# Gate columns of linear attention in the narrow token-major product; index keys and attention keys projected by one tile

## The chip, the cores and the metric

The kernel runs on 1 core of one Trainium2 chip. The metric is the device time of one execution in microseconds (us). Three runs of the kernel before gave 2982.54, 2981.31 and 2982.35 us, median 2982.35.

## What is computed

One transformer block over 2048 tokens of width 1024. What matters here is its first half, cut to the lines that count:

```python
a = rms_norm(h, g_mix)
(gq, gk, gv, gg, ga, dq, dk, dv, iq, ik, iw, sq, sk, sv) = split(a @ w_in)   # 2520 columns
# gla: ga has 16 columns a token and goes through a small matrix to the decay
log_a = log_sigmoid(ga @ w_alpha2 + b_alpha) / GLA_TAU
# dsa: for every block of 128 queries, the 256 keys with the best index score
rel = relu(einsum('bthd,bsd->bths', iq, ik)); score = einsum('bth,bths->bts', iw, rel)
_, sel = top_k(score, 256)
logits = einsum('bthd,btkd->bhtk', dq, dk[sel]) + bias        # softmax, times dv[sel]
# swa: a window of 128 keys, with sq, sk, sv
h = h + concat([gla, dsa, swa]) @ w_out
```

`ik` and `dk` have 64 columns each and are one vector per token, shared by all heads. A mixture of experts and a gated embedding follow; the change doesn't touch them.

## The kernel before, in words

**First stage, `project_and_select` (lines 112 to 858).** TensorE (PE) makes `a @ w_in` as a list of products, `products` (lines 196 to 201). A product ("f", m, c) is feature-major: weight tile m (up to 128 columns of `w_in`, stationary) against a chunk c of 512 tokens of the transposed activations `aT` (moving), 8 matmuls over the depth, into one of two PSUM buffers `psP`. A product ("t", ...) is token-major: 128 tokens stationary, weight columns moving. The first 36 products (tiles `FIRST`, and the narrow product of 200 columns: `dv`, `iw`, `sv`) go chunk by chunk. Then come the tiles `LATER` (11 tiles, 4 chunks each, 44 products), then 32 token-major products of 256 columns (`gv` for 16 token tiles, then `gg`). Tile 0 holds the 64 index-key columns twice, tile 5 the 64 attention-key columns twice, so that each key lies in both partition halves (the matmuls at lines 697 and 1398 use a half for each of two heads). Tile 15 is the gate tile: 16 columns.

ScalarE (ACT) copies each product out of PSUM (lines 540 to 557): keys to `kI` and `kA` in SBUF, the others to `stage`, from where SyncE (SP) stores them to `proj_f` or `proj_t` in HBM. Product i waits until product i - 2 is copied (line 657).

Between products PE runs the **score pieces** ("R", line 697): index queries against `kI`, up to 512 keys. ACT applies relu (line 567) and the two head weights (line 581), GpSimd (POOL) adds (lines 495 and 498). There are 152 pieces; from product 18 on up to 5 of them follow each product.

VectorE (DVE) finds each query's 256th score by a **bit search**, four query blocks at a time, in four groups: 31 steps, each counting the scores above a threshold (lines 766 to 797). In the second half of group 2 and in all steps of group 3, ACT counts for two of the four blocks (`sense`, lines 592 and 596, item "C"); DVE then waits for ACT's count at line 794. The order of ACT's copies, pieces and counts is written out in advance by `deal()` (lines 263 to 342) from a table of costs. Then `select` (lines 841 to 849) makes the mask, and POOL stores it to HBM (line 529). After all products PE, ACT and the ACT queue make six tiles of the gated embedding ("embed", lines 713, 722, 626, 628, 630), and SP loads what the second stage needs (`MixerLoads.ahead`, lines 909 to 938), into the SBUF region `home` in which `aT` had been.

**Second stage, `mixers` (lines 945 to 1680).** One list of items for all engines, merged from three streams: sparse attention (`stream_a`), window attention (`stream_w`) and linear attention (`stream_g`), each spread evenly over the same number of slots. Item ("g", r, 0) multiplies the gate columns of 512 tokens (`low`, 16 partitions, loaded by `load_g`, line 920) by `w_alpha`; the rest of `g` computes decays. PSUM use goes round five banks, `psX`.

Of the kernel before, what the change touches and what calls it, by code (L numbers as in the profile page):

```python
# [51 lines left out]
FM = [(0, C_GQ, 128), (128, C_GK, 128), (256, C_GA, 16), (272, C_DQ, 128), (400, C_DQ + 128, 128),  # L52
      (528, C_DK, 64), (592, C_IQ, 128), (720, C_IQ + 128, 128), (848, C_IQ + 256, 128),
      (976, C_IQ + 384, 128), (1104, C_IK, 64), (1168, C_SQ, 128), (1296, C_SQ + 128, 128),
      (1424, C_SQ + 256, 128), (1552, C_SQ + 384, 128), (1680, C_SK, 128)]
F_GQ, F_GK, F_GA, F_DQ, F_DK, F_IQ, F_IK, F_SQ, F_SK, NFM = 0, 128, 256, 272, 528, 592, 1104, 1168, 1680, 1808

T_GV, T_GG, T_DV, T_IW, T_SV, NTM = 0, 256, 512, 576, 584, 712


def bucket_ranges():
# [16 lines left out]
FIRST = [(None, ((C_IK, 64), (C_IK, 64)))] + [(F_IQ + 128 * i, ((C_IQ + 128 * i, 128),)) for i in range(4)]  # L78
LATER = ([(None, ((C_DK, 64), (C_DK, 64)))] + [(F_DQ + 128 * i, ((C_DQ + 128 * i, 128),)) for i in range(2)] + [(F_SQ + 128 * i, ((C_SQ + 128 * i, 128),)) for i in range(4)]
         + [(F_SK, ((C_SK, 128),)), (F_GQ, ((C_GQ, 128),)), (F_GK, ((C_GK, 128),)), (F_GA, ((C_GA, 16),))])  # L80
# [31 lines left out]
def project_and_select(nc, outer, keep, home, x, g_mix, w_in, rel_bias, proj_f, proj_t, mask_dram, bias_rows, ident, ident_ready, layer_in, w_ple, e_dram, e_squares, prefetch):  # L112
# [3 lines left out]
    with body as ctx:  # L116
# [14 lines left out]
        with early:  # L131
            xt = sb("xt", [P, NX, D], stack=early)
            w_iq3 = sb("w_iq3", [P, KD, P], stack=early)
            w_tm = sb("w_tm", [P, KD, 200], stack=early)
# [6 lines left out]
        stage_sv = sb("stage_sv", [P, 2, SKV * HD])  # L141
# [56 lines left out]
        for c in range(NCH):  # L198
            products += [("f", m, c) for m in range(5)] + [("t", 512, 200, c * TPC + t) for t in range(TPC)]
        FIRST_N = len(products)  # L200
        products += [("f", 5 + m, c) for m in range(len(LATER)) for c in range(NCH)]
        products += [("t", h * 256, 256, t) for h in range(2) for t in range(NT)]
# [57 lines left out]
        def deal():  # L260
# [6 lines left out]
            def on_pe(k):  # L267

                nonlocal pe_at, next_pe
                while next_pe <= k:  # L270
# [3 lines left out]
                    elif kind == "M":  # L274
                        p = products[i]
                        pe_at = max(pe_at, act_done.get(("M", i - 2), 0.0)) + (6.9 if p[0] == "f" else 2.8 if p[2] == 200 else 3.5)
# [30 lines left out]
            while k < len(order) or ahead:  # L307
# [24 lines left out]
                if kind == "M":  # L332
                    act_at += 0.65 if products[i][0] == "f" else 0.45
# [24 lines left out]
        def _(sp):  # L358
# [33 lines left out]
            for i, p in enumerate(products):  # L392
                if p == ("t", 512, 200, 0):
                    for t in range(3 * NX, NT):
                        load_x(t)
# [9 lines left out]
                elif p[0] == "t" and p[2] == 200:  # L405
                    t = p[3]
                    sp.dma_start(proj_t[ts(t, P), T_SV:T_SV + SKV * HD], stage_sv[:, t % 2, :]).then_inc(sv_stored[t % 2], 16)
# [5 lines left out]
                if p[0] == "f" and p[2] == NCH - 1:  # L413
# [5 lines left out]
                    elif m == len(tiles) - 2:  # L419
                        sp.dma_start(wide(0), w_columns(C_GV, 256)).then_inc(w_loaded[0], 16)  # L420
                    elif m == len(tiles) - 1:
                        sp.dma_start(wide(1), w_columns(C_GG, 256)).then_inc(w_loaded[2], 16)
# [110 lines left out]
        def _(act):  # L533
# [6 lines left out]
            def copy(i):  # L540
                p = products[i]
                act.wait_ge(mm_done, i + 1)
                if p[0] == "f" and i not in through:
                    act.activation((kI if p[1] == 0 else kA)[:, p[2] * CH:(p[2] + 1) * CH], psP[:, i % 2, :], ACT.Copy).then_inc(copied, 1)
# [4 lines left out]
                elif p[2] == 200:  # L549
# [4 lines left out]
                    act.activation(stage_sv[:, t % 2, :], psP[:, i % 2, HD + IH:200], ACT.Copy).then_inc(copied, 1)  # L554
# [86 lines left out]
        def _(pe):  # L641
# [11 lines left out]
            def product(i):  # L653
# [15 lines left out]
                else:  # L669
                    _, c0, n, t = p  # L670
                    if n == 200:
                        if t == 0:
                            pe.wait_ge(w_tm_loaded, 48)
# [3 lines left out]
                    for k in range(KD):  # L677
                        if n == 200:
# [2249 lines left out]
```

## Time and profile before

| | |
|---|---|
| median of three runs | 2982.35 us |
| span of the profiled execution, first to last instruction | 2979.8 us |
| device time of the profiled execution | not given apart; the three runs lie 1.5 to 2.7 us above its span |
| PE busy | 2686.2 us, 90% of the span |
| DVE, ACT, POOL busy | 1818.7, 1280.5, 952.8 us |
| mean granted TensorE clock | 0.954 of full speed |
| first stage | 0 to 887 us |
| second stage | 887 to about 1470 us |

A line of the timeline shows start and duration in us, the engine, the line of the kernel, the operation, output <- input, the count, and in brackets how long the engine had been idle before, with what ended the wait. "SPq" and "ACTq" are DMA issues. In the view of groups by line a row ends with the summed busy time, the mean duration in ns, and the idle time before. The view of windows gives the busy time of each engine in each stretch, with its number of instructions, then the granted clock.

### The profile page before, as it was taken

The page shows a single profiled execution, that of the slowest core. Times are in us where ns is not written, and L with a number is a line of the kernel's source. Part 1 is how long each engine was busy: PE and PEld are TensorE (multiplying, and loading weights), DVE is VectorE, ACT ScalarE, POOL GpSimd, SP SyncE. Part 2 cuts the span into 40 slices and gives each one's busy share as a digit, 9 for nine tenths or more (in the row PEclk, how much of TensorE's full clock was granted, in tenths as well). Part 3 has the DMA queues.
Part 4 walks back from the last instruction along what each step waited for, and adds up shares of the span by engine and source line. Part 5 has one row for each costly group of instructions (what it writes and reads, how often), then busy time and mean ns, then how long its engine had stood idle before and what let it go on. Part 6 is the DMA issues. An engine that isn't in the chain of part 4 may idle for free. (4 is left out here: it accounts for less than half of the span.)

```text
span 2979.8 us, 34896 instructions
## 1 busy us (share of the span) xinstructions
PE 2686.2 (90%) x11088; PEld 1679.6 (56%) x11089; DVE 1818.7 (61%) x2274; ACT 1280.5 (43%) x2369; POOL 952.8 (32%) x935
## 2 busy tenths in 40 slices
PE   6989789999986888887699958999999999999998
PEld 3634333443853444444488836666666666665687
DVE  2187999588876657765422277764564445641676
ACT  2377868839935555665512232222222222222322
POOL 2477887300011111111100014543443334532321
PEclk9999889999997889998799979999999999999999
DMA  5102211111150221222344376995596555972563
GB/s 154 53 30 53 31 37 36 57 56 40 52 198 29 76 66 43 90 66 88 126 170 142 112 268 246 330 361 209 204 355 217 213 210 203 349 294 96 192 218 134
DMA packets 222018, 439.66 MB, mean 148 GB/s; under 512 B 23048, under 2 KB 91208, under 8 KB 221768
## 3 DMA queue, kind: packets, MB, share of 16 engines
q1 hardware_dynamic: 199656, 358.31, 35.1%
q0 software_dynamic: 13456, 47.85, 5.1%
q10 hardware_dynamic: 8784, 31.99, 2.6%
q8 instruction: 63, 1.03, 0.2%
q14 instruction: 59, 0.48, 0.1%
HBM read 332.19 MB, written 105.91 MB: 147 GB/s over the span
## 5 line engine op out<-in xcount | busy, mean ns | idle before, releaser
L2337 DVE CAST p_high<-p_low 128x2048 fp32r<-128x2048 f32 x128 | 200.6, 1568 | 392.9 <-PE p_psG L2431 293.2
L668 PE MATMUL p_psP<-home,p_ring 128*128 128x512 f32 (+1 forms) x960 | 422.0, 598 | 0.0
L2447 PE MATMUL p_psY<-p_wd,p_hT 128*128 x768 | 337.9, 593 | 2.0 <-ACT p_hT L2507 1.9
L2339 DVE TENSOR_TENSOR p_low<-p_low,p_high 128x2048 fp32r<-128x2048 f32 x128 | 321.8, 2514 | 4.4
L668 PEld LDWEIGHTS p_psP<-home,p_ring 128*128 128x128 f32 (+1 forms) x960 | 175.7, 185 | 242.9 <-issue 242.7
L2447 PEld LDWEIGHTS p_psY<-p_wd,p_hT 128*128 128x128 f32 x768 | 142.2, 190 | 163.7 <-issue 163.6
L2370 POOL TENSOR_TENSOR p_hid<-p_act_g,p_act_u 128x512 f32<-128x512 f32 x48 | 62.5, 1302 | 527.2 <-ACT p_act_u L2502 274.9
L697 PE MATMUL p_psI<-p_kI,p_qI 64*128 64x512 f32 (+3 forms) x608 | 150.4, 603 | 51.8 <-ACT p_relu L567 51.7
L2364 POOL TENSOR_TENSOR p_xT_low<-p_xT,p_xT_high 128x512 fp32r<-128x512 f32 x96 | 191.6, 2014 | 4.1 <-ACT p_xT L2492 4.1
L2429 PE MATMUL p_psG<-p_high,p_xT_high 128*128 128x512 f32 x384 | 170.7, 445 | 15.3 <-DVE p_low L2339 7.6
L766 DVE TENSOR_SCALAR_CACHE_REDUCE p_equal<-p_S_low,p_flip 128x512 uint8<-128x512 f32 (+4 forms) x139 | 168.7, 1214 | 0.0
L2429 PE MATMUL p_psU<-p_high,p_xT_high 128*128 128x512 f32 x384 | 157.5, 410 | 5.5 <-DVE p_low L2339 5.5
L581 ACT ACTIVATE p_relu<-p_relu,p_small 128x512 f32<-128x512 f32 (+3 forms) x266 | 161.4, 661 | 0.0
L567 ACT ACTIVATE p_relu<-p_psI 128x1024 f32<-128x1024 f32 (+3 forms) x152 | 136.9, 914 | 41.7 <-POOL p_S_high L498 15.9
L2513 ACT ACTIVATE p_y<-p_psY 128x512 f32<-128x512 f32 x96 | 57.4, 598 | 224.7 <-PE p_psY L2447 224.7
L2430 PE MATMUL p_psG<-p_low,p_xT_high 128*128 x384 | 153.5, 400 | 0.0
L2431 PE MATMUL p_psG<-p_high,p_xT_low 128*128 128x512 f32 x384 | 153.2, 399 | 0.0
L766 DVE TENSOR_SCALAR_CACHE_REDUCE p_above<-p_S_low,p_flip 128x384 uint8<-128x384 f32 (+4 forms) x139 | 150.6, 1083 | 3.3
L2430 PE MATMUL p_psU<-p_low,p_xT_high 128*128 x384 | 151.9, 395 | 0.0
L2431 PE MATMUL p_psU<-p_high,p_xT_low 128*128 128x512 f32 x384 | 151.8, 395 | 0.0
L1541 DVE SCALAR_TENSOR_TENSOR p_logits<-p_mask,p_psL 128x1024 f32<-128x1024 uint8 (+3 forms) x80 | 84.8, 1060 | 107.5 <-PE p_psL L1398 102.7
L2498 ACT ACTIVATE p_act_g<-p_psG 128x512 f32<-128x512 f32 x48 | 28.7, 599 | 264.9 <-PE p_psG L2431 264.9
(405 smaller groups left out, 5662.1 us busy)
## 6 DMA issues: line engine op xcount, KB each, us to landing
p_low<-in_w_expert_gate_dram SPq DMA_DIRECT2D x32, 2048.0 KB, 13.5
p_low<-in_w_expert_up_dram SPq DMA_DIRECT2D x32, 2048.0 KB, 17.4
p_wd<-in_w_expert_down_dram SPq DMA_DIRECT2D x32, 2048.0 KB, 10.7
y_dram<-p_y ACTq DMA_DIRECT2D x48, 512.0 KB, 8.0
p_xt<-in_x_dram SPq DMA_DIRECT2D x32, 512.0 KB, 4.5
y_dram<-p_clear SPq DMA_DIRECT2D x32, 512.0 KB, 4.6
proj_f<-p_stage SPq DMA_DIRECT2D x52, 256.0 KB, 2.3
p_ot<-o_dram SPq DMA_DIRECT2D x16, 512.0 KB, 4.7
```

Of the source, the lines that this page charges most:

```text
L567: act.activation(relu[:, n % NRELU, :, 0:c1 - c0], psI[:, n % NI, :, 0:c1 - c0], ACT.Relu).then_inc(relu_done, 1)
L581: act.activation(dst, src, ACT.Copy, scale=small[:, j, h:h + 1]).then_inc(weighed, 1)
L668: mm = pe.matmul(psP[0:n, i % 2, :], w, aT[:, k, c * CH:(c + 1) * CH], start=k == 0, stop=k == KD - 1)
L697: mm = pe.matmul(psI[:, n % NI, half, 0:c1 - c0], qI[r, b % 2, i, :], kI[r, c0:c1], start=True, stop=True)
L766: return dve.tensor_scalar((above, equal)[jj % 2][:, 0:W], scores_of(S_low, S_high, j), value, None, ALU.is_ge, ALU.add, accum_out=cnt[:, ...
L2337: dve.tensor_copy(high[:, m, k, :], low[:, par, m, k, :].bitcast(F32)).then_inc(high_done, 1)
L2339: dve.tensor_tensor(low[:, par, m, k, :], low[:, par, m, k, :].bitcast(F32), high[:, m, k, :].bitcast(F32), ALU.subtract).then_inc(w_split, 1)
L2364: pool.tensor_tensor(xT_low[:, k, :], xT[:, k, :], xT_high[:, k, :].bitcast(F32), ALU.subtract).then_inc(xT_split, 1)
L2429: pe.matmul(ps[:, :], xT_high[:, k, :], high[:, m, k, :], start=k == 0, stop=False)
L2430: pe.matmul(ps[:, :], xT_high[:, k, :], left, start=False, stop=False)
L2431: mm = pe.matmul(ps[:, :], xT_low[:, k, :], high[:, m, k, :], start=False, stop=k == KD - 1)
L2447: mm = pe.matmul(psY[:, c, :], hT[:, par, k, :], wd[:, bass.ds(at, 1), k, c * CH:(c + 1) * CH].rearrange("p a f -> p (a f)"), start=k == 0 ...
```

## The change

Tile 0 becomes one tile of 128 columns, the 64 index keys and the 64 attention keys. ACT copies its product with four activations of 64 partitions each: index keys into both halves of `kI`, attention keys into both halves of `kA`. The attention-key tile is gone from `LATER`. The gate columns leave the feature-major tiles too: they are the last 16 columns of the narrow token-major product, now 216 wide, and are stored to `proj_t` with `sv`. In the second stage a new item ("a", r) transposes them back (four PE transposes, one ACT copy of 16 partitions x 512 into `low`) before ("g", r, 0). `gg` is projected before `gv`. The costs in `deal()` are changed for the two copies. Core of the diff:

```diff
-FIRST = [(None, ((C_IK, 64), (C_IK, 64)))] + [(F_IQ + 128 * i, ((C_IQ + 128 * i, 128),)) for i in range(4)]
-LATER = ([(None, ((C_DK, 64), (C_DK, 64)))] + [(F_DQ + 128 * i, ((C_DQ + 128 * i, 128),)) for i in range(2)] + [(F_SQ + 128 * i, ((C_SQ + 128 * i, 128),)) for i in range(4)]
-         + [(F_SK, ((C_SK, 128),)), (F_GQ, ((C_GQ, 128),)), (F_GK, ((C_GK, 128),)), (F_GA, ((C_GA, 16),))])
+FIRST = [(None, ((C_IK, 64), (C_DK, 64)))] + [(F_IQ + 128 * i, ((C_IQ + 128 * i, 128),)) for i in range(4)]
+LATER = ([(F_DQ + 128 * i, ((C_DQ + 128 * i, 128),)) for i in range(2)] + [(F_SQ + 128 * i, ((C_SQ + 128 * i, 128),)) for i in range(4)]
+         + [(F_SK, ((C_SK, 128),)), (F_GQ, ((C_GQ, 128),)), (F_GK, ((C_GK, 128),))])
+NARROW = ((C_DV, 64), (C_IW, 8), (C_SV, 128), (C_GA, 16))
+NW = sum(n for _, n in NARROW)
...
-            products += [("f", m, c) for m in range(5)] + [("t", 512, 200, c * TPC + t) for t in range(TPC)]
+            products += [("f", m, c) for m in range(5)] + [("t", 512, NW, c * TPC + t) for t in range(TPC)]
...
-        products += [("t", h * 256, 256, t) for h in range(2) for t in range(NT)]
+        products += [("t", h * 256, 256, t) for h in (1, 0) for t in range(NT)]
...
-                        pe_at = max(pe_at, act_done.get(("M", i - 2), 0.0)) + (6.9 if p[0] == "f" else 2.8 if p[2] == 200 else 3.5)
+                        pe_at = max(pe_at, act_done.get(("M", i - 2), 0.0)) + (6.9 if p[0] == "f" else 3.0 if p[2] == NW else 3.5)
...
-                    act_at += 0.65 if products[i][0] == "f" else 0.45
+                    act_at += 2.4 if i not in through and products[i][0] == "f" else 0.65 if products[i][0] == "f" else 0.45
...
-            for c0, n in ((C_DV, 64), (C_IW, 8), (C_SV, 128)):
+            for c0, n in NARROW:
                 sp.dma_start(w_tm[:, :, at:at + n], w_columns(c0, n)).then_inc(w_tm_loaded, 16)
...
-                    sp.dma_start(proj_t[ts(t, P), T_SV:T_SV + SKV * HD], stage_sv[:, t % 2, :]).then_inc(sv_stored[t % 2], 16)
+                    sp.dma_start(proj_t[ts(t, P), T_SV:T_SV + SKV * HD + GR], stage_sv[:, t % 2, :]).then_inc(sv_stored[t % 2], 16)
...
-                    act.activation((kI if p[1] == 0 else kA)[:, p[2] * CH:(p[2] + 1) * CH], psP[:, i % 2, :], ACT.Copy).then_inc(copied, 1)
+                    for h, keys in ((0, kI), (1, kA)):
+                        for half in range(2):
+                            ins = act.activation(keys[half * HD:(half + 1) * HD, p[2] * CH:(p[2] + 1) * CH], psP[h * HD:(h + 1) * HD, i % 2, :], ACT.Copy)
+                    ins.then_inc(copied, 1)
...
-        for dst, row, n in (("gq", F_GQ, P), ("gk", F_GK, P), ("low", F_GA, GR)):
-            sp.dma_start(self.tiles[dst][:, b, :], self.proj_f[row:row + n, c]).then_inc(self.loaded["g"][b], 16)
+        for dst, row in (("gq", F_GQ), ("gk", F_GK)):
+            sp.dma_start(self.tiles[dst][:, b, :], self.proj_f[row:row + P, c]).then_inc(self.loaded["g"][b], 16)
+        sp.dma_start(self.tiles["lowT"][:, b, :, :], self.proj_t[c, T_GA:T_GA + GR].rearrange("(j p) d -> p j d", p=P)).then_inc(self.loaded["g"][b], 16)
...
-        stream_g = [("g", 0, i) for i in range(7)] + [("s", 0)]
+        stream_g = [("a", 0)] + [("g", 0, i) for i in range(7)] + [("s", 0)]
...
+            if quarter + 1 < NQ and within == 0:
+                extra.append(("a", quarter + 1))
...
+                elif kind == "a":
+                    until_filled(act, item)
+                    act.activation(low[:, item[1] % 2, :], bank(item)[0:GR, :], ACT.Copy).then_inc(empty(item), 1)
...
+                elif kind == "a":
+                    r = item[1]
+                    pe.wait_ge(g_loaded[r % 2], 48 * (r // 2 + 1))
+                    until_empty(pe, item)
+                    for k in range(TPC):
+                        mm = pe.transpose(bank(item)[0:GR, k * P:(k + 1) * P], lowT[:, r % 2, k, :], ident[:, :])
+                    mm.then_inc(full(item), 1)
                 elif kind == "g" and item[2] == 0:
                     r = item[1]
                     if r == 0:
                         pe.wait_ge(g_const, 48)
-                    pe.wait_ge(g_loaded[r % 2], 48 * (r // 2 + 1))
+                    until_read(pe, ("a", r))
                     until_empty(pe, item)
```

## Rows read from the trace of the kernel before

**Rows 1.** Windows: busy time of each engine by stretch, then granted clock.
```profile
600.00:700.00 100.00, 100.00 (x234) 44.27 (x233) 86.78 (x112) 47.08 (x71) 2.98 (x4) 1.00 0.16 53
...
887.00:1467.00 580.00, 460.96 (x2540) 247.33 (x2540) 369.75 (x510) 331.86 (x770) 81.74 (x111) 0.89 0.21 65
```
**Rows 2.** Timeline, end of the first stage and start of the second.
```profile
854.07 0.38 ACT L557 ACTIVATE p_stage<-p_psP 128x256 f32<-128x256 f32 x1 [3.07 <-PE p_psP L683]
...
874.06 2.35 DVE L849 SCALAR_TENSOR_TENSOR p_S_high<-p_S_high,p_flip,p_equal 128x2048 uint8<-128x2048 f32 x1
...
876.70 0.54 POOL L529 DMA_DIRECT2D mask_dram<-p_S_high  x1 [11.73 <-DVE p_S_high L849]
...
879.41 0.33 ACTq L630 DMA_DIRECT2D e_dram<-p_ring  x1
...
886.96 0.81 SPq L1153 DMA_DIRECT2D p_mask<-mask_dram  x2
```
**Rows 3.** DMA issues, with KB and us to landing: 839 to 850, then 876 to 887.
```profile
mask_dram<-p_S_high POOLq DMA_DIRECT2D x1, 208.0 KB, 2.9
...
e_dram<-p_ring ACTq DMA_DIRECT2D x2, 512.0 KB, 6.5
...
mask_dram<-p_S_high POOLq DMA_DIRECT2D x1, 256.0 KB, 5.9
```
**Rows 4.** Timeline, DVE: search group 2 meets its first shared count.
```profile
524.39 0.08 DVE L766 DVE_READ_ACCUMULATOR p_equal<-p_S_low,p_flip 128x1 f32 x1
544.08 0.17 DVE L794 TENSOR_SCALAR p_psX<-p_cnt 128x4 int32<-128x4 f32 x1 [19.60 <-ACT p_cnt L596]
```
**Rows 5.** Timeline, ACT: rounds of one product and five pieces, then the first count.
```profile
521.73 0.60 ACT L548 ACTIVATE p_stage<-p_psP 128x512 f32<-128x512 f32 x1 [0.82 <-PE p_psP L668]
...
535.15 0.60 ACT L548 ACTIVATE p_stage<-p_psP 128x512 f32<-128x512 f32 x1 [0.84 <-PE p_psP L668]
...
540.49 1.46 ACT L592 ACTIVATE p_rank<-p_S_low,p_flip 128x1408 uint8<-128x1408 f32 x1
```
**Rows 6.** Timeline, ACT: copies of two feature-major products of 128 columns.
```profile
654.00 0.60 ACT L548 ACTIVATE p_stage<-p_psP 128x512 f32<-128x512 f32 x1 [6.27 <-PE p_psP L668]
660.86 0.60 ACT L548 ACTIVATE p_stage<-p_psP 128x512 f32<-128x512 f32 x1 [6.27 <-PE p_psP L668]
```
**Rows 7.** Timeline, DVE: group 3, ends of the counts of bits 25, 5, 4 and 3.
```profile
693.26 0.17 DVE L794 TENSOR_SCALAR p_psX<-p_cnt 128x4 int32<-128x4 f32 x1 [1.71 <-ACT p_cnt L596]
...
796.63 0.17 DVE L794 TENSOR_SCALAR p_psX<-p_cnt 128x4 int32<-128x4 f32 x1 [1.17 <-ACT p_cnt L596]
801.47 0.17 DVE L794 TENSOR_SCALAR p_psX<-p_cnt 128x4 int32<-128x4 f32 x1 [0.49 <-ACT p_cnt L596]
806.99 0.17 DVE L794 TENSOR_SCALAR p_psX<-p_cnt 128x4 int32<-128x4 f32 x1 [1.16 <-ACT p_cnt L596]
```
**Rows 8.** Timeline, ACT: copies of two token-major products of 256 columns.
```profile
843.71 0.38 ACT L557 ACTIVATE p_stage<-p_psP 128x256 f32<-128x256 f32 x1 [3.07 <-PE p_psP L683]
847.16 0.38 ACT L557 ACTIVATE p_stage<-p_psP 128x256 f32<-128x256 f32 x1 [3.07 <-PE p_psP L683]
```
**Rows 9.** Timeline, start of the kernel: narrow weights, then tokens, on SP's queue.
```profile
13.83 5.20 SPq L386 DMA_DIRECT2D p_w_tm<-in_w_in_dram  x3
...
24.81 1.06 ACT L537 ACTIVATE p_relu<-p_xt 128x1024 f32<-128x1024 f32 x1 [14.23 <-DMA p_xt<-in_x_dram]
```
**Rows 10.** Groups by line, ACT, first stage: copies of products.
```profile
L544 ACT ACTIVATE p_kI<-p_psP 128x512 f32<-128x512 f32 x4 | 2.4, 598 | 24.4 <-PE p_psP L668 24.4
...
L548 ACT ACTIVATE p_stage<-p_psP 16x512 f32<-16x512 f32 x4 | 2.3, 574 | 1.3 <-PE p_psP L668 1.3
```
**Rows 11.** Timeline, PE, pieces beside the narrow products: wait for ACT.
```profile
214.69 1.13 PE L697 MATMUL p_psI<-p_kI,p_qI 64*128 64x512 f32 x4 [1.85 <-ACT p_relu L567]
```
**Rows 12.** Second stage: PE transposes by line; then PE's longest waits.
```profile
L1473 PE MATMUL p_psX<-ident,p_oTW 128*128 128x128 f32 x64 | 10.9, 295 | 5.2 <-ACT p_oTW L1340 5.2
...
PE p_psX L1409 <- ACT p_logits L1301: 26.4, 12, 8.3
```

More of the change, by code:

```diff
@@ L50 @@
 C_SQ, C_SK, C_SV = 1752, 2264, 2392
[L52 to L58, printed above, removed]
+F_GQ, F_GK, F_DQ, F_IQ, F_SQ, F_SK, NFM = 0, 128, 256, 512, 1024, 1536, 1664
+T_GV, T_GG, T_SV, T_GA, NTM = 0, 256, 512, 640, 656
+NARROW = ((C_DV, 64), (C_IW, 8), (C_SV, 128), (C_GA, 16))
+NW = sum(n for _, n in NARROW)
 def bucket_ranges():
@@ L133, in project_and_select @@
             w_iq3 = sb("w_iq3", [P, KD, P], stack=early)
-            w_tm = sb("w_tm", [P, KD, 200], stack=early)
+            w_tm = sb("w_tm", [P, KD, NW], stack=early)
         S_high = sb("S_high", [P, sum(width(j) for j in range(LOW, NT))])
@@ L140, in project_and_select @@
         stage = sb("stage", [P, NSTAGE, CH])
-        stage_sv = sb("stage_sv", [P, 2, SKV * HD])
+        stage_sv = sb("stage_sv", [P, 2, SKV * HD + GR])
         qI = sb("qI", [P, 2, IP, P])
@@ L392, in _ @@
             for i, p in enumerate(products):
-                if p == ("t", 512, 200, 0):
+                if p == ("t", 512, NW, 0):
                     for t in range(3 * NX, NT):
@@ L404, in _ @@
                     sp.dma_start(proj_f[r0:r0 + n, ts(p[2], CH)], stage[0:n, q % NSTAGE, :]).then_inc(stored[q % NSTAGE], 16)
-                elif p[0] == "t" and p[2] == 200:
+                elif p[0] == "t" and p[2] == NW:
                     t = p[3]
-                    sp.dma_start(proj_t[ts(t, P), T_SV:T_SV + SKV * HD], stage_sv[:, t % 2, :]).then_inc(sv_stored[t % 2], 16)
+                    sp.dma_start(proj_t[ts(t, P), T_SV:T_SV + SKV * HD + GR], stage_sv[:, t % 2, :]).then_inc(sv_stored[t % 2], 16)
                 elif p[0] == "t":
@@ L419, in _ @@
                     elif m == len(tiles) - 2:
+                        sp.dma_start(wide(1), w_columns(C_GG, 256)).then_inc(w_loaded[2], 16)
+                    elif m == len(tiles) - 1:
                         sp.dma_start(wide(0), w_columns(C_GV, 256)).then_inc(w_loaded[0], 16)
-                    elif m == len(tiles) - 1:
-                        sp.dma_start(wide(1), w_columns(C_GG, 256)).then_inc(w_loaded[2], 16)
                 if i == len(products) - 8:
@@ L548, in copy @@
                     act.activation(stage[0:n, through[i] % NSTAGE, :], psP[0:n, i % 2, :], ACT.Copy).then_inc(copied, 1)
-                elif p[2] == 200:
+                elif p[2] == NW:
                     t = p[3]
@@ L553, in copy @@
                         act.wait_ge(sv_stored[t % 2], 16 * (t // 2))
-                    act.activation(stage_sv[:, t % 2, :], psP[:, i % 2, HD + IH:200], ACT.Copy).then_inc(copied, 1)
+                    act.activation(stage_sv[:, t % 2, :], psP[:, i % 2, HD + IH:NW], ACT.Copy).then_inc(copied, 1)
                 else:
@@ L670, in product @@
                     _, c0, n, t = p
-                    if n == 200:
+                    if n == NW:
                         if t == 0:
-                            pe.wait_ge(w_tm_loaded, 48)
+                            pe.wait_ge(w_tm_loaded, 16 * len(NARROW))
                     elif t == 0:
@@ L677, in product @@
                     for k in range(KD):
-                        if n == 200:
+                        if n == NW:
                             w = w_tm[:, k, :]
@@ L892, in mixer_home @@
     tiles = dict(kS=view(P, L), vS=view(P, NT, SKV * HD), nearA=view(P, AH, 2 * P), nearW=view(P, SH, 2 * WIN), qS=view(P, 2, SG, P), qA=view(P, 2, AH // 2, P),
-                 gq=view(P, 2, CH), gk=view(P, 2, CH), low=view(GR, 2, CH), gv=view(P, 2, TPC, HV), gate=view(P, TPC, HV), wa=view(GR, P), ba=view(P, 1), gn=view(P, GV),
+                 gq=view(P, 2, CH), gk=view(P, 2, CH), low=view(GR, 2, CH), lowT=view(P, 2, TPC, GR), gv=view(P, 2, TPC, HV), gate=view(P, TPC, HV), wa=view(GR, P), ba=view(P, 1), gn=view(P, GV),
                  sink=view(P, SH), sq=view(P, TPC, HV))
@@ L968, in mixers @@
         nearA, nearW, sink, kS, vS, qA, qS = (loads.tiles[n] for n in ("nearA", "nearW", "sink", "kS", "vS", "qA", "qS"))
-        gq, gk, low, gv, gate, wa, ba, gn = (loads.tiles[n] for n in ("gq", "gk", "low", "gv", "gate", "wa", "ba", "gn"))
+        gq, gk, low, lowT, gv, gate, wa, ba, gn = (loads.tiles[n] for n in ("gq", "gk", "low", "lowT", "gv", "gate", "wa", "ba", "gn"))
         mask = sb("mask", [P, 2, L], U8)
@@ L1110, in mixers @@
                 uses = 0
-            if item[0] == "g" and item[2] == 0:
+            if item[0] == "a" or (item[0] == "g" and item[2] == 0):
                 uses = 1
```

## The prediction

> **What bounds the kernel now.** I read the windows first. In the first stage PE is full from 600 us on, but DVE and ACT are nearly as busy, and in the second stage PE is busy for 461 of 580 us [rows 1]. So a full PE alone doesn't say that PE sets the end. The timeline of the hand-over does [rows 2]: the last product is copied at 854.5 us, and what ends the first stage is two later things side by side. DVE's last selection ends at 876.4 and its mask is stored; the embedding's last result is stored from 879.4. That store takes 6.5 us to land [rows 3], so it lands at 885.9, and the second stage begins at 886.96, 1.05 us after it. The mask's store would have let it begin a few us earlier. Both stores run beside SP's loads for the second stage, which can start only when `home` is free of the activations: 5.9 us for 256 KB against 2.9 us for 208 KB with the DMA engines free [rows 3].
>
> Then the chain that ends with DVE. In search group 2 DVE stood for 19.6 us until ACT counted [rows 4], because ACT's written order puts all 152 score pieces ahead of the first count. ACT got there at 540.5 [rows 5]. From there to the end, DVE and ACT alternate without slack, and ACT's order also holds them to PE's products. So the chain is: PE's products and pieces up to 540, then counts in step with products, then selection, mask, second stage. What changes the time is what moves 540.5, the pace of the counts, or the hand-over.
>
> **What is removed.** Eight feature-major products: four of attention keys, four of gate columns. One costs 6.87 us [rows 6], whatever its width (ACT's copy of 16 partitions follows the same pace), so PE sheds 55.0 us. All eight stand behind product 36. By the planner's list, worked through for the new kernel, the order up to the 72nd product is the old one: query tiles of the same cost take the places of the key tile, among the same pieces. Nothing ahead of 540.5 is therefore shed. From bit 25 of group 3 on, the counts now meet token-major products (3.45 us each [rows 8], three to two counts) where they met feature-major ones (three to four). Before, 20 counts from bit 25 to bit 5 took 103.4 us, 5.17 each; two counts beside three token-major products took 10.36 us, 5.18 each; one that waits for no product took 4.84 [rows 7]. So the pace stays, until products run out: the last four counts go at 4.84 in place of 20.7 / 4 = 5.18. **Gain 1.3 us.** PE's products then end some 50 us before DVE does.
>
> **What is added ahead of 540.5.** First, a fourth load of narrow weights: 1024 rows of 64 bytes, queued on SP ahead of the tokens that ACT waits 14.23 us for. The three loads there take 5.20 us of SP's queue [rows 9], 1.73 each, each with 1024 rows though of 256, 32 and 512 bytes. I take 1.7; it can't be under nothing. PE has work from the first tokens only, so it starts its products that much later. The Trainium skill ("DMA: Bandwidth & Descriptors", Measured) gives 0.95 us for a 64 KB transfer and calls those below it descriptor-dominated; by that figure the sum would be 0.8 us smaller. The rows here, with a time that doesn't follow the bytes, decide.
>
> Second, the narrow products: 16 columns more on 8 matmuls. From 256 to 512 columns a product grows by 6.87 - 3.45 = 3.42 us [rows 6, 8], 13.3 ns per column, so 16 columns cost 0.21 us, sixteen times 3.4 us. In the third and fourth chunk five pieces follow each narrow product and PE waits for ACT anyway (1.85 us once [rows 11]), so six of them are hidden: **2.1 us**, bounds 0 and 3.4. If that cover goes they cost the other 1.3.
>
> Third, the copies of tile 0: four in place of one. 16 partitions took 574 ns, 128 took 598 [rows 10], so 64 don't take half: three more of about 0.55 to 0.6, 1.6 to 1.8 us per product. The first two meet an idle ACT and a PE with two PSUM buffers: nothing. Those of chunks three and four are followed by pieces whose relu is queued behind them on ACT; PE may run two pieces ahead and then waits for them, and POOL waits for both. **3.2 us**, bounds 0 and 4 x 1.8 = 7.2.
>
> Does the loop of pieces soak this up? One product and five pieces take 13.42 us on ACT's clock [rows 5]; PE, ACT and POOL wait for each other in it, all start later by the same time, and no deadline from outside stands in it. So the shift comes through: 1.7 + 2.1 + 3.2 = **7.0 us**. DVE's own searches before are shielded by those 19.6 us.
>
> **The hand-over.** DVE ends at 876.4 + 7.0 - 1.3 = 882.1. The embedding starts when ACT is through its counts (some 30 us earlier than now, relative to DVE's end) and is out of the way, and SP's loads are too. The mask's issue follows by 0.3, landing takes 2.9 (bounds 2.9 and 5.9), the start 1.05: 886.35, against 886.96: **-0.6 us**. The 6.3 us of relief here pay for the shift.
>
> **The second stage.** Added: 16 transposes of 128 moving columns at 295 ns [rows 12], 4.7 us of PE, and four copies at 0.57, 2.3 us of ACT. PE is busy 79% of the stage [rows 1]; by that share 3.7 us show. Nothing (or less, since the linear stream's 96 items now lie wider) is one bound, 4.7 + 2.3 = 7.0 the other. The wait of PE for ACT's copy stands 17, 14 and 14 items behind its transposes in quarters 2 to 4 and only 4 in the first, where both engines wait at the start anyway. The loads of `lowT`, 512 rows of 64 bytes, come quarters ahead. The order of `gg` and `gv` and the addresses in `home` and `proj_t` move no wait.
>
> **Sum.** -0.6 + 3.7 = +3.1 us: the span goes from 2979.8 to 2982.9, and the median, 2.55 above the span, from 2982.35 to **2985.5 us**. A measurement of this kernel can tell about 0.2%, 6 us, from no change, so this is no change.
>
> **Rivals.**
> 1. *PE is the bound after all.* Then 55.0 - 3.4 - 7.0 = 44.6 us fall away: 2937.8. For it: PE at 100% for 300 us. Against it: DVE ends 22 us after the last product, and PE waits at the end, not DVE. 3%.
> 2. *The shift is soaked up in the pieces.* Then the hand-over's relief and the faster tail show: -1.3 - 6.3 = -7.6, and with the second stage's cost at its lower bound 2974.7. For it: ACT and PE both have idle time there. 15%.
> 3. *Slower: the score pieces take the whole of it.* Place: ACT's queue before the first count. Price: 1.7 + 3.4 + 7.2 = 12.3, less 1.3, less 6.3, plus 3.7: +8.4, 2990.8. It decides once the first shared count starts over 9.9 us later than now. For it: POOL and ACT are close to full in that loop, so a late relu can push more than its own length. Against it: the first two copies find ACT idle. 28%.
> 4. *PE goes cold.* PE is now busy until the hand-over; after the change it stands still after its last product and again after the embedding. The embedding took 854.5 to 879.4, 24.9 us [rows 2]; at the lower of the two clock levels, 1.2 GHz, up to twice that, 49.8. From 827 that is 877, its last store lands at 883.5 at worst, just before the mask: 0 to 2 us, 2988. The Trainium skill ("TensorE: Matmul & The Clock Gate", Part 1) says that idle time halves the clock and sustained work restores it; no row quoted here shows it at this place. 5%.
>
> **How the numbers follow.** The forecast has 49%. No change within 0.2% (2976.4 to 2988.3) holds the forecast and rival 4: 0.54. Faster holds rivals 1 and 2: 0.18. Slower is rival 3: 0.28. The range leaves rival 1 out and covers both bounds of the hand-over and of the second stage: 2975 to 2993.
>
> **What would show it.** Right: the first shared count at 547 to 548 instead of 540.5; the wait at line 794 near 26 us; the last product copied near 806; the last selection at 882, its mask landing in some 3 us, the second stage at about 886.5; the second stage 3 to 4 us longer. The forecast is wrong if the first shared count moves by under 3 or over 10 us, or if the second stage changes its length by over 7.

## The result and the profile after

The changed kernel takes **2993.42 us** (median of 5 runs, 2987.61 to 2995.08) against 2981.42 us of the kernel before beside it: ratio 1.0039, 95% interval 1.0027 to 1.0050. In a second series it took 2992.30 us against 2981.43: 1.0037 (1.0026 to 1.0049). The forecast was 2985.5 us (2975 to 2993) and no change; the time lies just above the upper end of its range, and the change is slower by 11 to 12 us. One kernel's runs differ by some 10 us each way (the kernel before: 2968 to 2988 over the series below), so single profiles are read by their rows up to the second stage, and medians of 4 to 12 runs beyond it.

The page of the kernel after, its span and busy times:

```profile
span 2992.2 us, 34668 instructions
PE 2638.6 (88%) x10976; PEld 1662.9 (56%) x10977; DVE 1818.2 (61%) x2274; ACT 1282.5 (43%) x2376; POOL 946.8 (32%) x935
```

The products that fell away are gone from PE, and the span is 12.4 us longer all the same. The chain of the prediction goes through the first shared count, so the reader goes there first. The timeline of ACT of the kernel after: the copies of products 36 to 41 out of PSUM, and the first shared count (start, length, then in brackets the idle time before it and what ended it):

```profile
358.63 0.60 ACT L550 ACTIVATE p_stage<-p_psP 128x512 f32<-128x512 f32 x1 [0.83 <-PE p_psP L670]
374.38 0.57 ACT L550 ACTIVATE p_stage<-p_psP 128x512 f32<-128x512 f32 x1
386.54 0.60 ACT L550 ACTIVATE p_stage<-p_psP 128x512 f32<-128x512 f32 x1 [2.15 <-PE p_psP L670]
414.64 0.60 ACT L550 ACTIVATE p_stage<-p_psP 128x512 f32<-128x512 f32 x1 [17.48 <-DMA proj_f<-p_stage]
430.62 0.60 ACT L550 ACTIVATE p_stage<-p_psP 128x512 f32<-128x512 f32 x1 [4.62 <-PE p_psP L670]
443.62 0.60 ACT L550 ACTIVATE p_stage<-p_psP 128x512 f32<-128x512 f32 x1 [1.88 <-PE p_psP L670]
...
553.65 1.46 ACT L594 ACTIVATE p_rank<-p_S_low,p_flip 128x1408 uint8<-128x1408 f32 x1
```

The count starts 13.2 us later than before [rows 5], where the forecast had 7.0. One copy stands out: it waited **17.48 us for a DMA**, a store of `stage` to `proj_f`. All three stage buffers were full: product 39 takes the buffer of product 36 again. The same copies in the kernel before:

```profile
350.91 0.60 ACT L544 ACTIVATE p_kA<-p_psP 128x512 f32<-128x512 f32 x1 [1.68 <-PE p_psP L668]
366.66 0.57 ACT L544 ACTIVATE p_kA<-p_psP 128x512 f32<-128x512 f32 x1
381.11 0.60 ACT L544 ACTIVATE p_kA<-p_psP 128x512 f32<-128x512 f32 x1 [3.48 <-PE p_psP L668]
392.57 0.60 ACT L544 ACTIVATE p_kA<-p_psP 128x512 f32<-128x512 f32 x1 [0.56 <-PE p_psP L668]
411.29 0.60 ACT L548 ACTIVATE p_stage<-p_psP 128x512 f32<-128x512 f32 x1
430.44 0.60 ACT L548 ACTIVATE p_stage<-p_psP 128x512 f32<-128x512 f32 x1 [5.12 <-PE p_psP L668]
```

The line of code says why it is new. Before, the first later tile was the attention keys, four products copied into `kA`: they need no stage buffer and no store. After, its place is taken by a tile of queries, which needs both. What stands in front of those stores, in SP's queue of the kernel after (the last line is the issue of product 36's store alone):

```profile
346.78 0.82 SPq L398 DMA_DIRECT2D bias_rows<-p_rows_a  x1
347.64 9.88 SPq L398 DMA_DIRECT2D bias_rows<-p_rows_s  x1
359.25 31.35 SPq L403 DMA_DIRECT2D proj_f<-p_stage  x1
```

The two transfers of the relative bias have 4 and 8 heads as their outermost dimension, 2.25 MB in all. Product 36's store took 31.35 us only to be issued behind them. DMA issues of the kernel after (KB each, median us to landing), first for 350 to 370 us, then for 370 to 430:

```profile
proj_f<-p_stage SPq DMA_DIRECT2D x1, 256.0 KB, 55.3
```

```profile
proj_f<-p_stage SPq DMA_DIRECT2D x4, 256.0 KB, 22.9
p_qI<-proj_f POOLq DMA_DIRECT2D x2, 256.0 KB, 10.7
```

and the same two stretches of the kernel before:

```profile
p_qI<-proj_f POOLq DMA_DIRECT2D x1, 256.0 KB, 18.1
```

```profile
proj_f<-p_stage SPq DMA_DIRECT2D x1, 256.0 KB, 2.2
p_qI<-proj_f POOLq DMA_DIRECT2D x1, 256.0 KB, 3.2
```

The bias transfers run some 65 us in both kernels: by the DMA rates along these stretches until about 405 us before and 413 after. Before, no store met them, only a load of `qI` (18.1 us to landing) and one of weights. After, three stores did, those of products 36 to 38. They took 55.3, 24.6 and 21.3 us to land, all at about 415 us, when the bias was through; the fourth took 3.3. The loads of `qI` come from GpSimd's own queue. One of them met the bias in either kernel and took 18.1 us both times, against 3.2 and 3.4 for those that didn't; 10.7 is the median of two. So the bias slows transfers of another queue too, but those behind it on SP's queue far more. The Trainium skill ("DMA: Bandwidth & Descriptors", Rules for kernel authors) says that DMAs issued from different engines run on the same 16 DMA engines and interleave; the 18.1 us of the load agree with that. Another queue for the bias wasn't tried. By an estimate from these rows it might have been enough: a store that lands in the 18.1 us of the load would have been through at 377 us, and ACT wanted its buffer at 397.

At the end of the first stage (timeline of the kernel after: embedding's last store, last selection, its mask's issue, second stage):

```profile
860.31 0.33 ACTq L632 DMA_DIRECT2D e_dram<-p_ring  x1
...
885.88 2.35 DVE L851 SCALAR_TENSOR_TENSOR p_S_high<-p_S_high,p_flip,p_equal 128x2048 uint8<-128x2048 f32 x1
...
888.53 0.54 POOL L528 DMA_DIRECT2D mask_dram<-p_S_high  x1 [11.73 <-DVE p_S_high L851]
...
893.82 0.81 SPq L1158 DMA_DIRECT2D p_mask<-mask_dram  x2
```

Against [rows 2] the selection is 11.8 us late and the second stage 6.9: the embedding is long out of the way, as foreseen.

### The profile page after: what moved, and what is told of

Same layout as the page of the kernel before. It is cut to its first block and busy times, and to the rows that moved or that the text cites. A ratio compares the mean times of both kernels' runs of the same rounds, so it can differ in the third digit from the quotient of the medians.

```text
span 2992.2 us, 34668 instructions
## 1 busy us (share of the span) xinstructions
PE 2638.6 (88%) x10976; PEld 1662.9 (56%) x10977; DVE 1818.2 (61%) x2274; ACT 1282.5 (43%) x2376; POOL 946.8 (32%) x935
## 5 line engine op out<-in xcount | busy, mean ns | idle before, releaser
L670 PE MATMUL p_psP<-home,p_ring 128*128 128x512 f32 x832 | 367.4, 600 | 0.0
L670 PEld LDWEIGHTS p_psP<-home,p_ring 128*128 128x128 f32 x832 | 157.6, 192 | 205.1 <-issue 204.9
L2444 PE MATMUL p_psG<-p_high,p_xT_high 128*128 128x512 f32 x384 | 170.6, 444 | 15.7 <-DVE p_low L2354 8.0
L1406 PE MATMUL p_psL<-p_kA,home 64*128 64x512 f32 (+3 forms) x320 | 95.0, 673 | 69.2 <-ACT home L1289 36.3
## 6 DMA issues: line engine op xcount, KB each, us to landing
p_low<-in_w_expert_up_dram SPq DMA_DIRECT2D x32, 2048.0 KB, 17.2
```

The source lines that it names most:

```text
L670: mm = pe.matmul(psP[0:n, i % 2, :], w, aT[:, k, c * CH:(c + 1) * CH], start=k == 0, stop=k == KD - 1)
L2444: pe.matmul(ps[:, :], xT_high[:, k, :], high[:, m, k, :], start=k == 0, stop=False)
```

## The experiments

Three kinds: what blocks the stores, what each half of the change costs, and what the second stage adds. All were timed beside the kernel before on the same chip.

**Twelve transfers in one go.** The idea was that a transfer by heads keeps few DMA engines busy, and one head's 128 rows would use all.

```
-    sp.dma_start(bias_rows[h0:h0 + n, :, :], rows[:, :].unsqueeze(1).broadcast_to([n, P, 384]))
+    for h in range(n):
+        sp.dma_start(bias_rows[h0 + h:h0 + h + 1, :, :], rows[h:h + 1, :].unsqueeze(1).broadcast_to([1, P, 384]))
```

> The changed kernel, with the rows of the relative bias stored head by head (12 transfers of one head's 128 rows each) in place of two transfers of 4 and 8 heads. Theory S: the first later tile is now a tile of queries whose results must be stored; its stores stand on SP's queue behind the two slow bias transfers, and ACT's copy of product 39 waited 17.5 us for a free stage buffer. Then that wait falls under 2 us, the first shared count starts at 549 us or earlier (after: 553.7), and the time is 2982 to 2989 us. Rival C: the shift comes from ACT's four copies per merged product and the narrow products, and the store's wait only showed where the loop had slack. Then the first shared count stays at 552 to 554 and the time at 2991 to 2995 us. Rival P: GpSimd's slow spell beside VectorE's selection sets the pace there. Then the wait moves to GpSimd's masks, and the time falls by under 3 us.

> The kernel before, with the same 12 transfers. Theory S: its first later tile is the keys, which need no store, so nothing waits for the bias transfers but the loads of queries (18.1 us to landing at that place); where they don't decide, the time stays at 2979 to 2983 us, and if they do, up to 11.4 us go (two products there are 18.7 and 19.2 us apart and not 13.2): 2970 us. Rival C: 2979 to 2983 us. Rival P (GpSimd beside VectorE's selection): the two distances of 18.7 and 19.2 us stay, 2979 to 2983 us.

Measured: **3010.39 us** for the changed kernel (ratio 1.0099, 1.0084 to 1.0115), and 2980.62 for the kernel before (1.0000, 0.9991 to 1.0009). No theory had 3010, so my mending failed, but it failed at the disputed place. ACT's timeline of the changed kernel with this edit:

```profile
437.14 0.60 ACT L551 ACTIVATE p_stage<-p_psP 128x512 f32<-128x512 f32 x1 [38.70 <-DMA proj_f<-p_stage]
```

The bias's DMA issues in 370 to 430 us of the same kernel, and its window (last columns: PE's clock, DMA share, GB/s):

```profile
bias_rows<-p_rows_s SPq DMA_DIRECT2D x7, 192.0 KB, 24.9
...
370.00:430.00 60.00, 27.09 (x87) 10.71 (x85) 58.82 (x91) 21.40 (x36) 29.02 (x24) 0.80 0.86 33
```

The DMA engines are now 86% busy and move 33 GB/s, where the kernel after moves 61 GB/s at a share of 0.34. That stretch of the kernel after holds its late stores too. In stretches in which almost nothing but the bias moves, it is 27 GB/s at a share of 0.86 (360 to 380 us) against 50 GB/s at 0.44 (360 to 370) and 24 GB/s at 0.22 (400 to 412) in the kernel after. A head's rows all come from one partition, and one head after another was slower than the two transfers side by side, though no slower than one of them. SP's queue was held by the issues of the bias until 419.5 us; only then was product 36's store issued. ACT's wait ended at 437.1 us and not at 414.6, its length grew from 17.5 to 38.7 us, and the first shared count from 553.7 to 575.6 us. In the kernel before the same slower transfers cost nothing. So the wait follows the bias transfers, and only where a staged tile stands behind them.

**Taking the transfers apart.** One head behind each of the 12 products from product 36 on, so that a store meets at most one.

```
+    h = i - FIRST_N
+    if 0 <= h < AH + SH:
+        row = rows_a[h:h + 1, :] if h < AH else rows_s[h - AH:h - AH + 1, :]
+        sp.dma_start(bias_rows[h:h + 1, :, :], row.unsqueeze(1).broadcast_to([1, P, 384]))
```

> The changed kernel once more, unaltered, beside runs of the kernel before on the same chip as the next three. Theory S, additive: against the kernel before it should lose what its parts show (gate_only -6.0 us, keys_only -3.6 us by medians) unless the parts interact; from the first stage's rows alone (second stage 6.9 us later, second stage 3.0 us longer) +10 us. If it lands at +8 us or more again, the parts do interact or the first five runs were typical; if at +4 or less, the first median was an unlucky draw of runs that vary by 9 us each way.

> The changed kernel, with the bias rows stored one head at a time, one behind each of the 12 products from product 36 on, so that no store of a product waits for more than one of them (192 KB, some 7 us, and products are 13 us apart). Theory S: the wait of ACT's copy at product 39 goes from 17.5 us to under 2 us, the first shared count from 553.7 to 544 to 547 us, the second stage starts at 885 to 888 us and not at 893.8, and the time falls by 6 to 9 us against after_again. Rival C (ACT's copies alone): the first shared count stays at 552 to 554 us and the time within 2 us of after_again. Rival P (GpSimd beside VectorE's selection holds products 39 to 41 in any case): the first shared count at 549 to 551 us, 3 to 4 us of gain.

Measured: after_again 2992.30 us; after_bias_spread **2980.09 us** (ratio to the kernel before 0.9997, 0.9987 to 1.0007), 12.2 us less. Unaltered in another series:

> after_bias_spread unaltered, beside the next three on the same chip: 2978 to 2982 us.

It took 2979.45 us (0.9999, 0.9989 to 1.0009). ACT's timeline of after_bias_spread, the copy of product 39 and the first count:

```profile
400.25 0.60 ACT L552 ACTIVATE p_stage<-p_psP 128x512 f32<-128x512 f32 x1 [1.22 <-PE p_psP L672]
...
543.90 1.46 ACT L596 ACTIVATE p_rank<-p_S_low,p_flip 128x1408 uint8<-128x1408 f32 x1
```

and its DMA issues in 370 to 430 us:

```profile
proj_f<-p_stage SPq DMA_DIRECT2D x4, 256.0 KB, 2.4
...
bias_rows<-p_rows_a SPq DMA_DIRECT2D x2, 192.0 KB, 8.9
```

The stores land in 2.4 us, the wait is gone, the count starts at 543.9 and not at 555.2 (after_again), and 11.3 us earlier at the count become 12.2 in the time. Counted from product 36 to the count, which leaves out how the start varies, it is 12.0 us in both pairs of profiles (195.0 us in the two of the kernel after, 183.1 in the two with this edit). Theory S stands and C and P fall. This one wait accounts for the whole slowdown. Whether it is the place on SP's queue or the sharing of the DMA engines that makes the store late is not told apart by this: the edit changes both.

> The kernel before, with the bias rows stored one head behind each of 12 products. Theory S: no product is stored at that place, so there is nothing to gain: within 3 us of the kernel before. Rival: the spread itself is what gains in keys_only_spread (-10.7 us against the kernel before); then 2971 to 2974 us.

It took 2979.20 us (0.9996, 0.9983 to 1.0008): the spread alone gains nothing.

**Half of the change each.** gate_only keeps both key tiles as they were; keys_only keeps the gate columns as a feature-major tile.

```
 gate_only:
-FIRST = [(None, ((C_IK, 64), (C_DK, 64)))] + ...
+FIRST = [(None, ((C_IK, 64), (C_IK, 64)))] + ...
+LATER = ([(None, ((C_DK, 64), (C_DK, 64)))] + ...
 keys_only:
-NARROW = ((C_DV, 64), (C_IW, 8), (C_SV, 128), (C_GA, 16))
+LATER = (... + [(F_SK, ((C_SK, 128),)), (F_GQ, ((C_GQ, 128),)), (F_GK, ((C_GK, 128),)), (F_GA, ((C_GA, 16),))])
```

> Only the gate columns are moved; both key tiles are as before, so the first later tile is the keys again. Theory S: no wait for a stage buffer at product 39; the first shared count 2 to 3 us later than before (narrow products alone), 542 to 544 us, the second stage 3.0 us longer, the hand-over some 3 to 5 us shorter: 2980 to 2984 us. Rival C: the same at this place, since the four copies are away too. Were most of the loss in the narrow products or the second stage: 2988 us and more.

> Only the key tiles are merged; the gate columns are a feature-major tile as before. Theory S: the wait of ACT's copy for a stage buffer at product 39 is back at 15 us or more, the first shared count starts 10 us or more later than before (551 us or later), the hand-over gives 5 us back, the second stage is as before: 2984 to 2989 us. Rival C: the copies alone, first shared count 545 to 547 us, no wait over 5 us for a store, 2979 to 2983 us.

> gate_only with the bias rows stored one head behind each product. Theory S: with the key tile in the first later place no store waits for the bias rows, so spreading them gives nothing: 2973 to 2977 us, first shared count 539 to 541 us. It can only gain if the loads of queries and weights that were slow beside them (3 to 16 us to landing) held anything up.

> gate_only unaltered. Its first series gave 2974.9 us, and with the bias rows spread 2979.5 us. If spreading does nothing here, both are draws of one kernel: 2975 to 2979.5 us, and moving the gate columns alone is worth 0 to 5 us. If spreading costs 4 us, it is 2974 to 2976 us again.

Measured: gate_only 2974.93 us (0.9985, 0.9974 to 0.9996), in the second series 2979.90 (0.9996, 0.9985 to 1.0007), with the spread 2979.53 (1.0001, 0.9988 to 1.0015); by the ratios of the three it gains 0 to 5 us. keys_only 2977.37 (0.9989, 0.9978 to 1.0000). The first shared counts of gate_only and of keys_only, and the copy before it that waits:

```profile
539.86 1.46 ACT L591 ACTIVATE p_rank<-p_S_low,p_flip 128x1408 uint8<-128x1408 f32 x1
```

```profile
411.38 0.60 ACT L551 ACTIVATE p_stage<-p_psP 128x512 f32<-128x512 f32 x1 [16.64 <-DMA proj_f<-p_stage]
...
550.61 1.46 ACT L595 ACTIVATE p_rank<-p_S_low,p_flip 128x1408 uint8<-128x1408 f32 x1
```

As theory S has it, the wait comes with the merged key tile and not with the gate columns. I had put the cost of it in keys_only too high: its time stayed below the kernel before although its count is 10 us later. gate_only came out under its expected 2980 to 2984 us in both series, with its count before the expected 542 to 544, and gate_only_spread above its 2973 to 2977.

**The merged tile without the wait.**

> Only the key tiles merged, and the bias rows stored one head behind each of 12 products. Theory S: first shared count 542 to 543 us in place of 550.6, second stage at 884 us in place of 892.3, 8 us less than keys_only, so 2969 us where the kernel before stands at 2981; less gain if the second stage's own spread hides it. Rival C: no change from keys_only, 2977 us.

> keys_only_spread unaltered, on the chip of the two beside it: 2967 to 2974 us if its 10.7 us are real, 2976 us or more if the first series was lucky.

Measured: 2970.75 us (0.9965, 0.9951 to 0.9978) and **2965.75 us** (0.9951, 0.9934 to 0.9968): faster than both kernels in both series.

**Two copies in place of four.**

```
-    for h, keys in ((0, kI), (1, kA)):
-        for half in range(2):
-            ins = act.activation(keys[half * HD:(half + 1) * HD, ...], psP[h * HD:(h + 1) * HD, i % 2, :], ACT.Copy)
+    for keys in (kI, kA):
+        ins = act.activation(keys[:, ...], psP[:, i % 2, :], ACT.Copy)
```

> As after_bias_spread, but the merged key tile is copied in two copies of 128 partitions and not four of 64: both halves of each key buffer then hold one tile each, so scores and logits are of mixed keys. It prices the four copies. By my reading of the first two traces (4.8 us of shift between gate_only and keys_only ahead of product 38, for three more copies per product), theory: two copies fewer give back 3 us, bounds 2.2 and 4.8; first shared count 541 to 545 us. Rival: a merged product costs by its later start of the pieces, not by ACT's time; then under 1 us.

It took 2973.36 us (0.9976, 0.9967 to 0.9985), 6.7 less than after_bias_spread, and its first count starts at 539.72, 4.2 us earlier. At the count that is near the upper bound that I had given (4.8); the time fell by more. The rows of the third chunk show where it goes. ACT's timeline of the kernel after, around the four copies, and of spread_two_copies:

```profile
154.32 1.19 ACT L545 ACTIVATE p_kI<-p_psP 64x512 f32<-64x512 f32 x2 [3.54 <-PE p_psP L670]
155.53 1.20 ACT L545 ACTIVATE p_kA<-p_psP 64x512 f32<-64x512 f32 x2
171.28 0.60 ACT L550 ACTIVATE p_stage<-p_psP 128x512 f32<-128x512 f32 x1 [6.10 <-PE p_psP L670]
```

```profile
155.02 0.60 ACT L546 ACTIVATE p_kI<-p_psP 128x512 f32<-128x512 f32 x1 [3.54 <-PE p_psP L671]
155.51 0.59 ACT L546 ACTIVATE p_kA<-p_psP 128x512 f32<-128x512 f32 x1
167.80 0.60 ACT L551 ACTIVATE p_stage<-p_psP 128x512 f32<-128x512 f32 x1 [3.43 <-PE p_psP L671]
```

From the first copy to the next product's copy it is 16.96 us with four copies and 12.78 with two; the kernel before, with one, had 12.78 too. So the second copy costs nothing here, and four cost 4.2 us more. Other profiles with four copies have 15.7 to 17.2 us there, and in the fourth chunk 14.1 to 17.2, where one or two copies have 12.78 again. PE's timeline shows what the 4.2 us are, kernel before, then after (pieces, pieces, the next product's 16 matmuls):

```profile
154.98 1.35 PE L697 MATMUL p_psI<-p_kI,p_qI 64*128 64x512 f32 x8 [0.90 <-ACT p_relu L567]
157.39 1.13 PE L697 MATMUL p_psI<-p_kI,p_qI 64*128 64x512 f32 x4 [1.05 <-ACT p_relu L567]
158.44 7.13 PE L668 MATMUL p_psP<-home,p_ring 128*128 128x512 f32 x16
```

```profile
157.82 1.35 PE L699 MATMUL p_psI<-p_kI,p_qI 64*128 64x512 f32 x8 [2.26 <-ACT p_relu L569]
160.23 2.08 PE L699 MATMUL p_psI<-p_kI,p_qI 64*128 64x512 f32 x4 [1.05 <-ACT p_relu L569]
162.24 9.01 PE L670 MATMUL p_psP<-home,p_ring 128*128 128x512 f32 x16
```

PE waited 1.4 us longer for a relu behind the copies (2.26 against 0.90). The pieces and the product after it took 2.8 us longer for the same matmuls (2.08 against 1.13, 9.01 against 7.13): from 150 to 165 us PE's clock was granted at 0.81 on average in place of 1.00. So two thirds of the 4.2 us are clock.

**The second stage's turning.** The items that turn the gate columns are left out, and 16 rows of other columns are loaded in the place of `low`, as the kernel before loads its gate rows; so the gates are wrong.

```
-    sp.dma_start(self.tiles["lowT"][:, b, :, :], self.proj_t[c, T_GA:T_GA + GR].rearrange("(j p) d -> p j d", p=P))
+    sp.dma_start(self.tiles["low"][:, b, :], self.proj_f[F_GK:F_GK + GR, c])
-    stream_g = [("a", 0)] + [("g", 0, i) for i in range(7)] + [("s", 0)]
+    stream_g = [("g", 0, i) for i in range(7)] + [("s", 0)]
```

> As after_bias_spread, but the second stage doesn't turn the gate columns: 16 feature-major rows of the keys of linear attention are loaded in their place, as the kernel before loads its gate rows (so the gates are wrong), and the 16 transposes, 4 copies and their waits are gone. The rest is the same. Theory A: the turning costs its share of PE, 3.7 us (bounds 0 and 7.0). Rival B: after_bias_spread and keys_only_spread stood 9.3 us apart though their second stages began only 0.85 us apart, so the turning (with its waits, its DMA of 64-byte rows, and the order that it gives the stream) costs 7 to 9 us. Rival N: the second stage varies so much from run to run that it costs under 2 us and the 9.3 us came from elsewhere.

> The same edit of the second stage on gate_only: Theory A 3.7 us less than gate_only (2974.9): 2971 us. Rival B: 2966 to 2968 us. Rival N: 2973 to 2976 us.

Measured: 2973.51 us, **5.9 us** less than after_bias_spread_2 beside it, and 2965.09 us, which is 9.8 less than the first series of gate_only and 14.4 less than gate_only_spread beside it. The first pair lies inside theory A's bounds (0 to 7.0) and under B, the second says B or more. The rows of the transposes and of their copies in the kernel after, second stage:

```profile
L1488 PE MATMUL p_psX<-ident,home 128*16 128x128 f32 x16 | 3.7, 375 | 1.1 <-DVE p_um L1672 1.1
```

```profile
L1348 ACT ACTIVATE home<-p_psX 16x512 f32<-16x512 f32 x4 | 2.3, 578 | 5.9 <-PE p_psX L1488 5.9
```

PE's busy time is 3.7 us where the forecast had 4.7, ACT's 2.3 as in the forecast. ACT stood 5.9 us in front of two of the four copies, 5.3 of it in front of one. The second stage's length is read between SP's first mask load and the first load of the mixers' output. It is 584.8 us on average in the nine profiles with turning (580.7 to 588.2) and 576.9 in the eight without (568.9 to 587.5): 7.8 us. Two of them, after_bias_spread_2 and keys_only_spread_2, SP's queue at the start, at the loads of the eighth and the fourteenth mask, and at the end:

```profile
883.08 0.81 SPq L1160 DMA_DIRECT2D p_mask<-mask_dram  x2
...
1136.57 0.85 SPq L1160 DMA_DIRECT2D p_mask<-mask_dram  x1
...
1374.37 0.47 SPq L1160 DMA_DIRECT2D p_mask<-mask_dram  x1
...
1468.39 0.32 SPq L1766 DMA_DIRECT2D p_ot<-o_dram  x1
```

```profile
886.88 0.82 SPq L1158 DMA_DIRECT2D p_mask<-mask_dram  x2
...
1135.07 0.46 SPq L1158 DMA_DIRECT2D p_mask<-mask_dram  x1
...
1362.78 0.47 SPq L1158 DMA_DIRECT2D p_mask<-mask_dram  x1
...
1455.80 0.32 SPq L1754 DMA_DIRECT2D p_ot<-o_dram  x1
```

The middle stretch takes 237.8 us with turning and 227.7 without it. In spread_no_turning it took 234.1, so not all of such a difference is the turning's. The edit also takes away the loads of `lowT`, which these runs don't tell apart from the turning.

## Why the prediction was wrong

**The step that failed** is the sentence on what is removed: "query tiles of the same cost take the places of the key tile, among the same pieces. Nothing ahead of 540.5 is therefore shed." It counted the moved tile by PE and by the planner's list, which knows neither SP nor a DMA. A moved tile brings its stores, and the key tile, whose place the query tile took behind the bias transfers, has none. The term missing ahead of the first count is 11.3 us (after_bias_spread against after_again), 12.2 in the time. It is more than the miss of 7 to 8 us: without it the time is 2980, some 5 under the forecast, so what the sum did hold was put too high by about as much.

**Startup, +1.7.** It was nothing. The four narrow loads took 6.21 us of SP's queue against 5.20 [rows 9], but ACT's next square came at 24.62 us against 24.81, and on average of eight profiles with four loads at 24.98 against 24.86 in six with three.

**Narrow products, +2.1.** Right: gate_only's copy of product 36 is 2.1 us later than the kernel before's (353.02 against 350.91; 2.5 on average of four profiles against three), with four narrow loads and nothing else changed ahead of it.

**Four copies, +3.2.** Too small. Two of the four copies were worth 4.2 us at the count of one pair; keys_only, without the narrow columns, has product 36 copied 4.8 us late. The mechanism was the one named (relu queued behind them, PE two pieces ahead), but PE's wait also cost it clock, which I had not priced there. The three terms together, 7.0, measured 7.7 at product 36 in the first profile (358.63 against 350.91) and 9.2 on average of six profiles against three. That 7.0 comes near is luck: the startup was too high, the copies too low.

**The pieces soak it up (rival 2).** In part, and "the shift comes through" was wrong to that extent. With the bias taken apart, product 36 is 9.8 us late and the first count 5.4 (two profiles against three of the kernel before's order), and the 17.5 us of the new wait became 12.0. All of it goes between products 36 and 41: from product 41 to the count it is 110.0 to 110.1 us in all 17 profiles, so there the loop is as rigid as forecast. In gate_only GpSimd ran slowly from 387 to 416 us beside VectorE's selection, as it did in the kernel before (an addition of 128x512 took 1.27 us elsewhere and up to 3.4 there), and products 39, 40 and 41 were copied 19.4 and 18.1 us apart, much as in the kernel before (18.7 and 19.2). After the change that stretch lay under the wait, and they were 16.0 and 13.0 apart. Why GpSimd is slow there was not tried.

**Tail, -1.3.** Right: the last counts of the kernel after stand 4.84 us apart, and VectorE's delay went from 13.2 to 11.8.

**Hand-over.** The embedding was out of the way and the mask alone decided, as foreseen. Its store landed in 2.3 us, but the start came 5.3 us after the issue and not 3.95, so the relief in the start was 5.0 and not 6.3. On the other side the second item follows after 13.6 us in every kernel that is freed of the embedding, and after 15.7 to 17.6 in the three whose product order is that of before, so some 3 us more (16.5 on average, less 13.6) were relieved than I had counted.

**Second stage, +3.7.** Too small: 5.9 us in one pair, more in the other, 7.8 on average of the profiles. PE's term alone was 1.0 us too high, so taking it by PE's share of busy time left something out. ACT's wait for the turning in its written order, 5.9 us, fits, but ACT's idle time was not shown to be what counts there.

**Rival 3** came out at nearly the right place and size (a count over 9.9 us late, 2990.8 us) by another mechanism, so its hit is luck: its copies and narrow products alone, 5.4 us at the count, stay under its point. At 28% it had been given less than the no-change case, and no rival had a DMA in it at all.

**What stays open.** keys_only_spread is 11 and 15 us faster than the kernel before, though its second stage begins only 0 to 4 us earlier (883.3 and 886.9 against 887.0) and has the same code. The rows give some 3 us by the freed mask loads; the rest lies in the pace of the second stage, which differs by up to 19 us between profiles of equal code. A sum for after_bias_spread doesn't close either: the first count comes at 543.4 us (two profiles) against 538.1 (three of the kernel before's order), +5.4, less 1.3 for the tail, 4.9 at the start and 2.9 at the second item, plus 5.9 for the turning: +2.2, where the medians show -1. What sets that pace was not tried. Nor was the bias on a queue other than SP's, which would have told the order on the queue from the sharing of the DMA engines.

## What to carry to other kernels

When work changes places, list for each moved step its queue, its buffers and its transfers, and look at what else is in flight at the new place: a step without a store may be what hides a slow transfer. A planner's list that knows compute engines alone can't show it. When a slow transfer can't be made faster, put its parts between the stores it would block: here that took back 12 us, and the merged key tile alone with this edit gives 2966 to 2971 us in place of 2981.

## What the runs showed of the hardware

- Two transfers whose source is a few partitions (192 KB from each, read 128 times) slowed every other transfer of 256 KB in flight. A store behind them on the same queue took 31.35 us to be issued and 55.3 to land, against 2.2 clear of them. A load from another queue took 18.1 us, against 3.2.
- Those two moved 50 GB/s together at a DMA share of 0.44, and 24 GB/s at 0.22 at the end. Taken apart into one head each, they moved 27 GB/s at 0.86. I had expected them to be faster. The Trainium skill ("DMA: Bandwidth & Descriptors", Rules for kernel authors) advises an outermost dimension whose size is a multiple of 16, at best the 128 partitions, so that all 16 DMA engines take part. The higher share agrees with more of them taking part, but the rate did not follow, so for this source the rule brought nothing. That the reads of one partition are the limit fits, but wasn't tried by itself. A head's transfer by itself took 8.9 us to land.
- ACT's copy of 64 partitions took 0.60 us, the same as 128 [rows 10]; the copies of a tile should be counted, not their partitions.
- A transpose of a 128x16 tile took 375 ns on average, but that is the clock and not the shape: the last four took 269 to 272 ns at a granted clock of 1.00, as those of 128x128 beside them did (272 to 273), and the twelve before them, at 0.50, mostly 417 to 421.
